# Two blocks of a network on one core: the loads of the expert weights in another order, and four half sums of the second output product made earlier

## The reference, cut to what matters

```python
def hier_moe(h, p):                       # first block, 16 experts of width 256
    ...                                   # combine: two experts of one group per token
    gate = jnp.einsum('td,edf->tef', t, p['w_gate'])
    up = jnp.einsum('td,edf->tef', t, p['w_up'])
    hid = jax.nn.silu(gate) * up * combine[..., None]
    return jnp.einsum('tef,efd->td', hid, p['w_down']).reshape(b, L, d)

# second block
    u = rmsnorm(h, norm_mix[i]) @ w_in[i]
    u_pool, u_ssm = u[..., :D_POOL], u[..., D_POOL:]          # 512 and 512 columns
    y_pool = pool_mixer(u_pool, w_pool[i], pool_scale[i])
    y_ssm = ssm_mixer(u_ssm, ...)   # y = gelu(scan + skip); y * sigmoid(y @ w_glu + b_glu)
    h = h + jnp.concatenate([y_pool, y_ssm], axis=-1) @ w_out[i]
    h = h + swiglu(rmsnorm(h, norm_ffn[i]), w_gate[i], w_up[i], w_down[i])
```

## Time and profile before

| | |
|---|---|
| runs shown, median | 3334.88 us |
| profiled execution | 3342.64 us |
| its span, first to last instruction | 3340.5 us |
| mean granted TensorE clock | 0.952 |
| PE busy | 3075.4 us, 92% |
| DVE busy | 1522.6 us, 46% |
| ACT busy | 754.1 us, 23% |
| POOL busy | 1059.2 us, 32% |
| bytes from DRAM | 231.98 MB, mean 77 GB/s |

### The profile page before, as it was taken

One profiled execution on the slowest core, in us unless ns is written; L12 is line 12 of the kernel. 1 busy time (PEld: TensorE's weight loads), 2 busy tenths in 40 slices (PEclk: granted clock), 3 DMA queues, 4 the chain that ended last, 5 costly groups with the idle time before them and its releaser, 6 DMA issues.

```text
span 3340.5 us, 28822 instructions
## 1 busy us (share of the span) xinstructions
PE 3075.4 (92%) x10281; PEld 1540.7 (46%) x10281; DVE 1522.6 (46%) x2470; ACT 754.1 (23%) x1568; POOL 1059.2 (32%) x982
## 2 busy tenths in 40 slices
PE   8996999998999999999698995697899999999996
PEld 4553554444455554444444442366444444444442
DVE  2433782345666665222433223539113444544446
ACT  1223854411233333011111111512211000000002
POOL 0002770000567767100000001245004444555445
PEclk8997999999999999999799998798899999999998
DMA  6000432001000000210588887101003111121101
GB/s 256 19 0 0 118 91 92 26 26 51 1 1 1 1 1 1 67 38 29 172 302 298 322 334 277 45 0 38 26 0 101 38 38 38 38 70 44 38 13 57
DMA packets 132990, 259.53 MB, mean 78 GB/s; under 512 B 24776, under 2 KB 80752, under 8 KB 120688
## 3 DMA queue, kind: packets, MB, share of 16 engines
q1 hardware_dynamic: 120304, 216.60, 18.6%
q0 software_dynamic: 6768, 24.64, 2.1%
q10 hardware_dynamic: 5776, 16.46, 1.2%
HBM read 231.98 MB, written 25.70 MB: 77 GB/s over the span
## 4 chain that ended last, share of the span: by engine, by line
PE 82%; DVE 7%; DMA 5%; issue 3%; POOL 1%; ACT 1%; SPq 0%; ACTq 0%; DVEq 0%; POOLq 0%
PE ps L3053 16%; PE ps L3069 7%; PE ps L1453 7%; PE ps L493 6%; PE ps L1045 5%; PE ps L1857 5%; PE ps L1222 5%; PE ps L1241 4%; DMA ring<-in_w_up 4%; PE ps L1257 4%; PE ps L956 3%; PE ps L2820 3%; PE ps L1876 2%; PE ps L2122 2%; PE ps L900 1%
## 5 line engine op out<-in xcount | busy, mean ns | idle before, releaser
L1334 DVE TENSOR_REDUCE arena_b<-ps 128x1 f32<-128x512 f32 (+1 forms) x384 | 217.3, 600 | 144.4 <-PE ps L1222 144.1
L3018 POOL TENSOR_TENSOR arena_b<-arena_b,arena_d 128x512 f32<-128x512 f32 x132 | 165.7, 1271 | 370.2 <-DVE arena_d L3178 368.7
L3156 DVE TENSOR_TENSOR arena_d<-arena_d,ps 128x512 f32<-128x512 f32 x154 | 102.0, 686 | 388.1 <-PE ps L3053 388.1
L1857 PE MATMUL ps<-ring,arena_a 128*128 128x512 f32 x496 | 237.6, 635 | 33.8 <-issue 18.0
L1316 POOL TENSOR_TENSOR arena_b<-arena_b 128x512 f32<-128x512 f32 x182 | 224.5, 1267 | 92.4 <-ACT arena_b L1298 92.4
L1222 PE MATMUL ps<-arena_d,arena_a 64*128 64x512 f32 (+1 forms) x768 | 234.9, 534 | 3.6 <-DVE arena_b L1325 2.9
L1241 PE MATMUL ps<-arena_a,arena_d 64*128 64x512 f32 x640 | 220.0, 607 | 2.4 <-ACT arena_b L1298 1.8
L3175 DVE TENSOR_TENSOR arena_b<-arena_b,ps 128x512 f32<-128x512 f32 x264 | 174.8, 685 | 50.9 <-POOL arena_b L3018 25.5
L1857 PEld LDWEIGHTS ps<-ring,arena_a 128*128 128x128 f32 x496 | 99.7, 204 | 168.1 <-issue 149.5
L493 PE MATMUL ps<-arena_b,ring 128*128 128x512 f32 x384 | 166.9, 592 | 0.7 <-ACT arena_t L472 0.7
L1045 PE MATMUL ps<-ring,arena_b 128*128 128x512 f32 x384 | 167.4, 592 | 0.0
(11 more groups left out here) (546 smaller groups left out, 5363.6 us busy)
## 6 DMA issues: line engine op xcount, KB each, us to landing
ring<-in_w_gate SPq DMA_DIRECT2D x42, 1024.0 KB, 7.8
ring<-in_w_up SPq DMA_DIRECT2D x42, 1024.0 KB, 10.4
ring<-in_w_down SPq DMA_DIRECT2D x42, 1024.0 KB, 6.8
ring<-in_w_in SPq DMA_DIRECT2D x10, 2048.0 KB, 15.3
ring<-in_w_mod SPq DMA_DIRECT2D x32, 512.0 KB, 4.0
yslots<-arena_a ACTq DMA_DIRECT2D x31, 512.0 KB
ring<-in_w_mod SPq DMA_DIRECT2D x4, 2048.0 KB, 13.9
ring<-in_w_out SPq DMA_DIRECT2D x4, 2048.0 KB, 7.8
```

Source lines behind the costliest of these rows:

```text
L1334: eng.tensor_reduce(mx3[j % 2][:, t, e, piece:piece + 1], ps[:, shared("s", u), 0:k1 - k0], AX.X, ALU.max).then_inc(s_mx, 1)
L1857: mm = eng.matmul(ps[:, s % 2, :], xsT[s % 2][:, k, :], sguw[s % 2][:, :, k, :], start=(k == 0), stop=(k == KT - 1))
```

## The change

There are two parts. In `sp_slots` the gate and up loads of slot s+1 are issued ahead of the down load of slot s. In the second block, the half of an output sum that reads the pooled columns (k 0 to 3) becomes a function of its own, `pe_out2_pooled`; it is called for sum 0 ahead of the last quarter's `states_i`, for sum 2 behind it, for sum 4 ahead of the last gelu turn, for sum 1 at the head of `pe_out2`, and for the other sums in their old place. The gate product moves to banks 4 to 7, the sums to banks by `out2_bank`, and k 4 to 7 of sum 0 wait for VectorE's gate multiplications one by one.

```diff
--- before.py
+++ after.py
@@ -1828,12 +1828,20 @@
 
             eng.wait_ge(s_wo, 2 * LT)
             eng.wait_ge(s_place, N_EIDX)
-            for s in range(NSLOT):
+
+            def first_weights(s):
                 e = eng.value_load(eidx[0:1, s:s + 1], min_val=0, max_val=NE - 1)
                 if s >= 2:
                     eng.wait_ge(gu_done, s - 1)
                 eng.dma_start(sguw[s % 2][:, 0], gate_of[e]).then_inc(gu_in[s % 2], 16)
                 eng.dma_start(sguw[s % 2][:, 1], up_of[e]).then_inc(gu_in[s % 2], 16)
+
+
+            first_weights(0)
+            for s in range(NSLOT):
+                if s + 1 < NSLOT:
+                    first_weights(s + 1)
+                e = eng.value_load(eidx[0:1, s:s + 1], min_val=0, max_val=NE - 1)
                 if s >= 2:
                     eng.wait_ge(dn_done, s - 1)
                 eng.dma_start(sdnw[s % 2], down_of[e]).then_inc(dn_in[s % 2], 16)
@@ -2613,6 +2621,23 @@
                                 kall.rearrange("p g h -> p (g h)"), start=True, stop=True)
             mm.then_inc(qp["inner"], 1)
 
+
+        def out2_bank(u):
+            return 0 if u == 0 else (3, 1, 0, 2)[(u - 1) % 4]
+
+        def pe_out2_pooled(eng, u):
+            t, n = u // 2, u % 2
+            eng.wait_ge(s_wo2[n], 16)
+            eng.wait_ge(s_pyc, 8)
+            eng.wait_ge(qv["inputs_i"], NQ)
+            if u >= 5:
+                eng.wait_ge(s_ffn, u - 3)
+            elif u == 3:
+                eng.wait_ge(s_ffn, 1)
+            for k in range(4):
+                eng.matmul(ps[:, out2_bank(u), :], ycat[:, k, t * P:(t + 1) * P], (wo5, slot(1))[n][:, k, :],
+                           start=(k == 0), stop=False)
+
         def pe_quarters(eng):
             def u_turned(q):
                 if q == 0:
@@ -2668,7 +2693,11 @@
             eng.wait_ge(qv["u_turned"], 2)
             pe_shifts(eng, 1)
             for q in range(NQ):
+                if q == NQ - 1:
+                    pe_out2_pooled(eng, 0)
                 states_i(q)
+                if q == NQ - 1:
+                    pe_out2_pooled(eng, 2)
                 if q + 2 < NQ:
                     eng.wait_ge(qv["inner"], q + 2)
                     pe_e_turned(eng, q + 2)
@@ -2683,6 +2712,7 @@
                     pe_shifts(eng, q + 2)
                 if q >= 1:
                     pe_gelu_turned(eng, q - 1)
+            pe_out2_pooled(eng, 4)
             pe_gelu_turned(eng, NQ - 1)
 
         def pe_gelu_turned(eng, q):
@@ -2775,7 +2805,7 @@
             for j in range(8):
                 eng.wait_ge(s_z, 2 * LT + j + 1)
                 m, h = j // 2, j % 2
-                eng.activation(sg[:, m, h * HALF:(h + 1) * HALF], ps[:, j % 4, :], ACT.Sigmoid,
+                eng.activation(sg[:, m, h * HALF:(h + 1) * HALF], ps[:, 4 + j % 4, :], ACT.Sigmoid,
                                bias=col("b_glu_2")[:, m:m + 1]).then_inc(s_zs, 1)
 
         def pe_glu(eng):
@@ -2786,7 +2816,7 @@
                 if j >= 4:
                     eng.wait_ge(s_zs, 2 * LT + j - 3)
                 for k in range(4):
-                    mm = eng.matmul(ps[:, j % 4, :], wglu[:, k, m * P:(m + 1) * P],
+                    mm = eng.matmul(ps[:, 4 + j % 4, :], wglu[:, k, m * P:(m + 1) * P],
                                     yt[:, k, h * HALF:(h + 1) * HALF], start=(k == 0), stop=(k == 3))
                 mm.then_inc(s_z, 1)
 
@@ -2802,10 +2832,7 @@
         ends["h2"] = [(s_ffn, 2 * LT)]
 
         def pe_out2(eng):
-            eng.wait_ge(s_zg, 2 * LT + 4)
-            eng.wait_ge(s_zs, 2 * LT + 8)
-            for n in range(2):
-                eng.wait_ge(s_wo2[n], 16)
+            pe_out2_pooled(eng, 1)
 
             def turn(t):
                 pe_turn_tile(eng, t, xr[t % 2], lambda t: eng.wait_ge(s_xr, LT + t + 1), 2 * LT)
@@ -2813,13 +2840,16 @@
             for t in range(LT):
                 for n in range(2):
                     u = 2 * t + n
-                    if u >= 4:
-                        eng.wait_ge(s_ffn, u - 3)
-                    for k in range(KT):
-                        src = ycat[:, k] if k < 4 else yt[:, k - 4]
-                        mm = eng.matmul(ps[:, u % 4, :], src[:, t * P:(t + 1) * P], (wo5, slot(1))[n][:, k, :],
-                                        start=(k == 0), stop=(k == KT - 1))
+                    if u not in (0, 1, 2, 4):
+                        pe_out2_pooled(eng, u)
+                    for k in range(4, KT):
+                        if u == 0:
+                            eng.wait_ge(s_zg, 2 * LT + k - 3)
+                        mm = eng.matmul(ps[:, out2_bank(u), :], yt[:, k - 4, t * P:(t + 1) * P],
+                                        (wo5, slot(1))[n][:, k, :], start=False, stop=(k == KT - 1))
                     mm.then_inc(s_o2, 1)
+                if t == 1:
+                    eng.wait_ge(s_zs, 2 * LT + 8)
                 if t >= 1:
                     turn(t - 1)
             turn(LT - 1)
@@ -2847,7 +2877,7 @@
                     u = 2 * t + n
                     cs = slice(n * HALF, (n + 1) * HALF)
                     eng.wait_ge(s_o2, u + 1)
-                    eng.tensor_tensor(x1[:, t, cs], x1[:, t, cs], ps[:, u % 4, :], ALU.add).then_inc(s_ffn, 1)
+                    eng.tensor_tensor(x1[:, t, cs], x1[:, t, cs], ps[:, out2_bank(u), :], ALU.add).then_inc(s_ffn, 1)
                 eng.wait_ge(s_ssq, LT + t + 1)
                 eng.tensor_scalar(ss8[:, 1, t:t + 1], ss8[:, 1, t:t + 1], 1.0 / D, EPS_RMS, ALU.mult, ALU.add
                                   ).then_inc(s_rv, 1)
```

## The result

The changed kernel takes 3303.99 us (median of 4, 3301.95 to 3304.8) against 3334.24 us (4 runs, 3328.01 to 3335.53): a ratio of 0.9912, 95% interval 0.9895 to 0.9929, so 30 us faster (24 to 35 by the interval); 3302 was predicted. Its profiled execution took 3304.77 us with a span of 3302.9. The spans of the two profiles differ by 37.6 us, more than the timed runs do.

| stretch | before | after | difference |
|---|---|---|---|
| start to first row turn of the slots | 1642.73 | 1640.42 | -2.3 |
| to gate/up of slot 15 | 207.24 | 206.39 | -0.9 |
| gate/up of slot 15 to that of slot 30 | 190.25 | 171.40 | -18.9 |
| to the gelu turn of quarter 1 | 287.69 | 287.05 | -0.6 |
| to the gate product | 24.79 | 29.86 | +5.1 |

The account below looks back on a forecast made before the run. TensorE, busy 92% of the span, was taken as the bound. Gains of 15.5 (loads), 2.5 (start) and 14.6 (pooled halves) sum to 32.6 us off 3334.9, giving 3302; the forecast's own range is 3298 to 3316, the overall range 3295 to 3319.

Parts of the forecast that it names:

- The weight waits: Expert slots after 1850: seven waits on up weights vanish with SP's new load order, gaining 15.5 us, range 10.7 to 18.8.
- the step to the median: Whole kernel: the median shown is 7.8 us below the profiled execution, taken to come from places outside the changed stretches.
- The six waits that stay: Expert slots before 1850: six waits called issue, 18.0 us, are ended by VectorE, so the change leaves them.
- (c): Slots before 1850: weights ended the six early waits too, so 18.0 us and some 7 of low clock go: 3277; chance 0.04.
- The start: Start of the slots: five loads issued instead of six, so the first slot starts 2.5 us earlier, range 0 to 2.9.
- The pooled halves: Last quarter, gate and output product: four half sums moved ahead gain 17.4 less 2.8, so 14.6 us, range 8.2 to 15.
- (a): Slots: memory is the bound, the rate stays at 326 GB/s and earlier issue only queues longer: 3318; chance 0.10.
- (b): Last quarter: the panel wait keeps the clock low into the gate product, eating the pooled halves' gain: 3319.7; chance 0.06.
- (e): Whole change does nothing, another wait of the same length standing behind each removed one: 3335; chance 0.03.
- (d): Slots: row stores starve behind weights, each of 29 slots losing 1.5 us if they land at 17.5: 3346; chance 0.03.

Follow-up runs that it names:

- run with six loads: Changed kernel with down of slot 1 loaded ahead of gate/up of slot 2 without a wait; first rows waited for 8.72 us, no total time given.
- the gate wait only: Changed kernel with no half sums ahead of the gate product, pooled halves of sums 0 and 1 filling the wait for the gate; 3307.93 us, single run.

## Why the prediction was right

**The weight waits.** Right in cause, place and count. All seven went and nothing took their place. One detail was misread: the down product that ended at 1849.97 and let the up load of 1851.69 go is that of slot 13, not 14; it is the one two slots back from the down load of slot 15 that stood ahead in SP's list, and the argument stands. What was off is the size: I took a period of 11.65 us, because I feared the rate (11.38 at 363 GB/s, 11.97 at 345). The rate was no limit: the stretch ran at 11.43. The rates that I read were those of a kernel that left the queues idle at times, and the run at 404 GB/s shows that they told what was asked for, not what could be had. I also leaned on two windows where the same trace had others: 377 GB/s over 1863 to 1871 and 369 over 1881 to 1891, so 363 was neither its highest rate nor its only window above 358.

```profile
1863.00:1871.00 8.00, 6.71 (x9) 2.86 (x10) 0.00 (x0) 0.00 (x0) 0.00 (x0) 0.57 0.96 377
1881.00:1891.00 10.00, 9.44 (x30) 4.55 (x28) 2.64 (x7) 1.89 (x5) 0.94 (x1) 1.00 0.97 369
```

The term was 15.5, the profile gave 18.9. That the timed gain of 30 us is still below 32.6 has another cause, the step to the median: I wrote that the 7.8 us between the profiled execution and the median came from places outside these stretches. A good part came from inside. On the mean of four profiles the old order cost 14.1 us, not 18.9. Both errors are near 4 us and go opposite ways, so that 3302 came within 2 us of the measured time is partly luck.

The Trainium skill (page "DMA: Bandwidth & Descriptors", section Specifications) gives about 358 GB/s as the limit of HBM per core. The changed kernel runs at just 358 over 171 us, which could pass for that limit, but the run with more stores holds 404 over the same passes, so the measurement speaks against the figure as a limit for this program, whose trace has one core at work.

**The six waits that stay.** Right: 18.0 us in both, put down to VectorE by the 0.1 us between the end of its modulation and the start of gate/up, and shown by moving VectorE's instructions. The chain that ended last goes through a weight load at the first of the six (and at five of them in all); it was a wait behind two things, and neither view names the later one. Rival (c) priced the low clock behind the six waits at some 7 us; it is 11.0 us in the changed kernel, and moving VectorE's constants gave 29.9 in all.

**The start.** 2.5 was taken. Between the two profiles it is 2.0 us of wait and 2.4 us up to gate/up of slot 2. The run with six loads has 1.6 us of wait and only 0.9 up to gate/up of slot 2, so 2.5 is at the upper end of what the runs show.

**The pooled halves.** Step by step, behind the gelu turn of quarter 1:

| | predicted | measured |
|---|---|---|
| half of sum 0 starts | 7.1 behind the turn's end | 6.9 |
| it takes | 6.1 | 5.8 to the next pass |
| gate product later by | 5.8 | 5.1 |
| gate product shorter by | 3.0 | 2.9 |
| behind the gate product | 17.4 | 17.6 |
| part 2 | 14.6 | 15.4 |

The 15.4 is the difference of two profiles. In the five profiles without early halves gelu turn to last row turn takes 179.9 to 181.6 us, 180.9 on the mean, and in the five with the halves of the changed kernel 166.0 to 166.2, so part 2 is 14.7 us on the mean. With 14.1 for the loads and about 2 for the start that is 31, near the 30 of the timed runs.

Two readings carried it. One is that a half put *ahead* of a pass on an in-order engine brings its own wait with it: the panel landed 3.3 us after the point at which the states pass had started before. The other is that filled pauses give back more than their length, since the clock stays at its high level behind them. Whether the gate product would keep it behind a pause of 2.1 us was a choice by a hair; in all five profiles with a half ahead of the last gelu turn and that pause of 2.08 us it did (27.73 us), and in the six without that half it did not (30.3 to 30.7). That the early halves are the cause is shown, since the run without them has the low clock again (30.64); whether it is the filled 3.03 us or the longer work before the pause is not.

Rivals: (a), (b) and (e) did not happen; (c) is refuted by the constants moved in both kernels; (d) by row stores that land in 4.0 us at the median and 4.3 at most in the changed kernel, and in 12.5 at most with twice as many.

**What stays open.** Why the old order waits 7 to 12 us by execution was not traced; the up loads landed in 10.1 to 10.6 us at the median in all three profiles. The kernels with a single run each (the gate wait only, six loads, more traffic) are judged by their traces, not by their times. It was not tried how far above 404 GB/s the slots would begin to wait.

## What to carry to other kernels

A queue that issues in order makes each load wait for every condition ahead of it: list the loads by when their buffer comes free, not by which slot they belong to. Where a wait has two conditions, removing the earlier one gives nothing and removing the later one gives only the distance to the next, so look for what ended within 0.1 us of the resume before believing the name in the view. Work moved forward as filler goes behind the pass on the critical path, not ahead of it, if it has a wait of its own.

## What the runs showed of the hardware

The slots' traffic reached 404 GB/s for 171 us on one core (weights in, rows in, rows out twice) at a DMA share of 0.99. Among the waits for weights, TensorE's clock fell to the low level behind pauses of 2.40 and 2.73 us and in the other profiles of before also behind 1.91, 2.07 and 2.08 us (gate/up 8.83 us each time), but not behind 1.96 us in one of them, nor behind the 2.08 us ahead of the gate product after: near 2 us the length of the pause alone does not tell. SP's load of the expert number took 1.27 us at the median where it stands behind the issues of gate and up (the one ahead of down in the new order, L1844) and 0.27 us where it stands behind the single issue of down (L1833). It cost next to nothing: down of a slot goes out 0.3 us behind the start of the next gate/up (1858.57 and 1858.23), where it was 0.2 us before (1850.16 and 1849.97).
